# Two rounded halves of an activation as one moving operand of 512 columns: the down and value products of a two-block transformer kernel

## The chip, the cores and the metric

The kernel runs on one core of a Trainium2 chip (trn2), in one launch. The metric is the device time in microseconds of that core. A lower number is better.

## The reference

Two blocks run one after the other on 256 tokens of width 1024, all in float32. The first has two layers of SwiGLU feed-forward, a mixer (a state-space mixer in layer 0, latent attention in layer 1) and a second feed-forward. The second has two layers of a recurrent mixer followed by a sparse feed-forward with 16384 experts. What the change touches are the products that end the four feed-forwards and the two expert layers:

```
def swiglu(h, w_gate, w_up, w_down):
    return (jax.nn.silu(h @ w_gate) * (h @ w_up)) @ w_down
...
        act = jax.nn.gelu(jnp.einsum('td,ted->te', hx, u_sel), approximate=False)
        return jnp.einsum('te,ted->td', gx * act, v_sel)
...
        x = x + FFN_RES_WEIGHT * mod[:, 0, 2][:, None, :] * swiglu(
            h, ffn_w_gate[i, 0], ffn_w_up[i, 0], ffn_w_down[i, 0])
```

`w_down` is 2816 x 1024. The kernel computes the expert layer densely: all 16384 rows of `peer_v` are multiplied, with a routing weight that is zero for most.

## The kernel before

Activations lie transposed: `x` is 8 tiles (d = 0 to 7) of 128 features by 256 tokens. All large weights come as one stream of blocks of 128 x 1024 float32 (512 KB), loaded by SyncE's queue (L480) in a written order into a ring of 4 buffers, or 12 in some stages. To keep float32 accuracy with TensorE's faster fp32r format, every block `W` is split in two: ScalarE rounds it (`split_hi`, L1146, into `weights_hi`, 4 buffers), VectorE computes the rest `W - rounded` in place (`split_lo`, L1641). Activations are split the same way. A product is then three matmuls: rounded x rounded, rounded x rest, rest x rounded.

There are ten stages s = 0 to 9. Each begins with a norm: ScalarE squares the 8 tiles of `x` as they are updated (L1129, waits on `x_upd`), TensorE sums them with a matrix of ones into bank 2 of PSUM (`norm_sum`, L498), ScalarE takes roots, VectorE the reciprocal and the scaled `h`. TensorE meanwhile writes zeros into banks 4 to 7 four times over (`open_acc`, L504, called in `front`), then takes the stage's first blocks.

Stages 0, 2, 3 and 5 are feed-forwards (`ffn`), with 22 pairs of gate and up blocks (`columns_in_parts`, L517, sums in banks 0 and 1 in turn) and then 22 down blocks (`rows_in_parts`, L550). ScalarE takes the silu of a gate sum (L1165), VectorE multiplies it with the up sum (L1674, counts `ffn_a`). For a down block the activation tile is rounded by ScalarE (`gate_hi`, L1159, into `small`) and the rest taken by VectorE (`gate_lo`, L1665, into `work`). VectorE also computes the modulation of later stages here, by products with `mod_weights` blocks (L1569) that POOL's queue loads. How many of these stand between two blocks is set by `products`: 56, 48, 48 and 72 per feed-forward.

Stages 7 and 9 are expert layers (`peer`), with 128 u blocks (L517, banks 0 to 3 in turn; ScalarE's gelu L1482 counts `pe_gelu` and SyncE stores the result to DRAM) and 128 v blocks in a hardware loop of four (`value`, L550). For each v block SyncE reads the activation back (L466), VectorE multiplies it with the routing weights (L2112), ScalarE rounds it (L1476), VectorE takes the rest (L2116). Before the v blocks TensorE writes zeros to banks 4 to 7 once (`open_acc`).

`rows_in_parts` runs over the 8 tiles d and adds three matmuls of 256 columns each to `acc[:, d, :]`, two tiles d per bank, in banks 4 to 7. In the last block of a stage it counts `acc_done` after d = 1, 3, 5. `residual` (L1635) then adds the 8 sums to `x`, times a modulation column, one VectorE instruction per tile, and counts `x_upd` after each. Stages 1, 4, 6 and 8 are the mixers, which the change leaves as they are. In stage 4, POOL's loads of constants and attention weights wait for all `x_upd` of stage 3.

Of the kernel before, what the change touches and what calls it, by code (L numbers as in the profile page):

```python
# [7 lines left out]
F32 = mybir.dt.float32  # L8
F32R = mybir.dt.float32r
# [260 lines left out]
def build(nc, stream, mods, cols_d, consts_d, x_d, pos_d, wuq_d, wukv_d, cond_d, keys_d, pool_d, lora_d, gup_d, vup_d, acts_d, out_d):  # L270
    with ExitStack() as ctx:
# [33 lines left out]

        work, (_, gat_lo) = sb_twice("work", [P, 2048], [([P, 1024], F32), ([P, 4, T], F32R)])

        small, (gat_hi, _) = sb_twice("small", [P, 5, T], [([P, 4, T], F32R), ([P, T], F32)])
        ijg, rs, rv = small[:, 0:3, :], small[:, 3, :], small[:, 4, :]
        PS = ctx.enter_context(nc.psum_tensor("psum", [P, 8, 512], F32))  # L310
        acc = PS[:, 4:8, :].rearrange("p b (s t) -> p (b s) t", s=2)
        sil = work[:, 0:1024].rearrange("p (b t) -> p b t", b=4)
        gat = work[:, 1024:2048].rearrange("p (b t) -> p b t", b=4)
# [175 lines left out]
        def _(pe):  # L489
# [10 lines left out]

            def open_acc():

                for b in range(4):
                    pe.matmul(PS[:, 4 + b, :], zeros[:, :], rep(zeros[:, :], 4), start=True, stop=False, skip_group_check=True)  # L504

# [39 lines left out]

            def rows_in_parts(w, wl, hi, lo, last=False):

                for d in range(DT):
                    for lhs, rhs in ((w, hi), (w, lo), (wl, hi)):
                        mm = pe.matmul(acc[:, d, :], lhs[:, d, :], rhs, start=False, stop=False, skip_group_check=True)  # L550
                    if last and d in (1, 3, 5):
                        mm.then_inc(sem["acc_done"], 1)
                mm.then_inc(sem["block_used"], 1)

            def ffn(s, f):
                base = BASE["ffn", f]
                front(s, ((PS[:, 0, 0:T], True), (PS[:, 0, T:2 * T], False), (PS[:, 1, 0:T], True)))
                for k in range(1, FT):
                    if k >= 2:
                        pe.wait_ge(sem["ffn_a"], FT * f + k - 1)  # L560
                    for half_ in range(1 if k == 1 else 0, 2):
                        w, wl = parts(base + 2 * k + half_)
                        columns_in_parts(PS[:, k % 2, half_ * T:(half_ + 1) * T], w, wl)
                for j in range(FT):
                    w, wl = parts(base + 2 * FT + j)
                    pe.wait_ge(sem["gate_lo"], GATES["ffn", f] + j + 1)
                    rows_in_parts(w, wl, gat_hi[:, j % 2, :], gat_lo[:, j % 4, :], j == FT - 1)

# [467 lines left out]
            def peer(l):  # L1036
# [40 lines left out]
                pe.wait_ge(sem["pe_wev"], T // 4 * (l + 1))  # L1077
                open_acc()

                def value(k, i, last=False):  # L1080
                    w, wl = parts(v0 + k, i)
                    pe.wait_ge(sem["gate_lo"], i * 4 + (GATES["uv", l] + k + 1))
                    rows_in_parts(w, wl, gat_hi[:, k, :], gat_lo[:, k, :], last)

# [455 lines left out]
        def _(dve):  # L1540
# [84 lines left out]
            def residual(s, last):  # L1625

                if s + 1 in FIRST:
                    for p in range(2):
                        split_lo(FIRST[s + 1] + p)
                for d in range(DT):  # L1630
                    if s in BY_ROWS and d < 6:
                        dve.wait_ge(sem["acc_done"], 3 * BY_ROWS.index(s) + d // 2 + 1)
                    else:
                        ready(last(d | 1))
                    dve.scalar_tensor_tensor(x[:, d, :], acc[:, d, :], modc[:, s, 16 + d:17 + d], x[:, d, :], ALU.mult, ALU.add)\  # L1635
                       .then_inc(sem["x_upd"], 1)

# [776 lines left out]
```

## Time and profile before

| | us |
|---|---|
| three timed runs | 3477.92, 3483.32, 3486.91 (median 3483.32) |
| span of the profiled execution, first to last instruction | 3476.7 |
| its own device time | not given apart; the three timed runs lie 1.2 to 10.2 above the span |
| TensorE busy with matmuls, of the span | 3342.0 (96%) |
| TensorE loading weights | 3203.1 (92%) |
| VectorE, ScalarE, POOL busy | 2579.5 (74%), 1608.5 (46%), 198.7 (6%) |
| mean granted TensorE clock | 0.987 of full speed |

How to read it: matmuls are pipelined, so the length that the profile shows for one (about 0.28 us) overlaps the next. What a matmul costs in a stream is the distance from one start to the next. In the chain of work that ended last, a piece "PE psum L550 x504" counts 504 records, matmuls and weight loads as the chain passes through them; its length over its count is the pace of one matmul.

### The profile page before, as it was taken

How to read it: one execution, taken by the hardware profiler on the slowest of the kernel's cores; microseconds unless marked ns; L12 is line 12 of the kernel's file. 1: busy time of each engine (PE TensorE's matmuls, PEld its weight loads, DVE VectorE, ACT ScalarE, POOL GpSimd, SP SyncE). 2: the span in 40 equal slices, each digit the busy share in tenths (PEclk: the TensorE clock that was granted, in tenths of full speed). 3: DMA queues.
4: the chain of work that ended last, by engine and by line, in shares of the span. 5: the costliest groups of instructions: out<-in, count | busy, mean ns of one | idle time of the engine just before them, and what ended most of it. 6: DMA issues, size and time to landing. Idle time of an engine off the chain costs nothing.

```text
span 3476.7 us, 68787 instructions
## 1 busy us (share of the span) xinstructions
PE 3342.0 (96%) x26804; PEld 3203.1 (92%) x26804; DVE 2579.5 (74%) x4576; ACT 1608.5 (46%) x2594; POOL 198.7 (6%) x331
## 2 busy tenths in 40 slices
PE   6999989999999998999999999999899999999998
PEld 5999869999967998889999999998789999999998
DVE  7889667888736896746977867776755977777776
ACT  3456644454445445134444444444414445444444
POOL 1100001101000220200000000000300000000000
PEclk9999999999999999999999999999999999999999
DMA  9964218979613993034664466665215665456665
GB/s 369 359 221 169 74 49 324 336 261 334 249 46 113 385 374 127 31 132 171 228 207 169 166 225 229 230 229 174 75 46 171 230 221 175 169 203 229 232 228 181
DMA packets 246578, 707.46 MB, mean 203 GB/s; under 512 B 27472, under 2 KB 93008, under 8 KB 244928
## 3 DMA queue, kind: packets, MB, share of 16 engines
q1 hardware_dynamic: 212112, 571.64, 47.2%
q0 software_dynamic: 34224, 132.46, 10.2%
q8 instruction: 167, 2.74, 0.3%
q14 instruction: 75, 0.61, 0.1%
HBM read 669.40 MB, written 34.60 MB: 202 GB/s over the span
## 4 chain that ended last, share of the span: by engine, by line
PE 85%; DVE 7%; DMA 4%; ACT 2%; issue 2%; SPq 0%; POOL 0%; DVEq 0%; ACTq 0%; POOLq 0%
PE psum L517 39%; PE psum L550 26%; PE psum L1074 3%; DMA ring<-stream 2%; PE psum L896 2%; PE psum L1009 1%; PE psum L647 1%; DVE ring L1641 1%; PE psum L916 1%; PE psum L498 1%; PE psum L529 1%; DMA arena<-mod_weights 1%; PE psum L530 1%; DVE arena L1569 1%; ACT weights_hi L1146 1%
## 5 line engine op out<-in xcount | busy, mean ns | idle before, releaser
L517 PE MATMUL psum<-hh,weights_hi 128*128 128x256 f32 x4216 | 1212.2, 288 | 19.2 <-ACT arena L1360 8.1
L1146 ACT ACTIVATE weights_hi<-ring 128x1024 fp32r<-128x1024 f32 x711 | 752.0, 1058 | 993.6 <-DMA ring<-stream 928.6
L517 PE MATMUL psum<-h,weights_hi 128*128 128x256 f32 x4216 | 1197.5, 284 | 0.0
L1641 DVE TENSOR_TENSOR ring<-ring,weights_hi 128x1024 fp32r<-128x1024 f32 x711 | 870.1, 1226 | 440.0 <-ACT weights_hi L1146 434.9
L517 PE MATMUL psum<-hh,ring 128*128 128x256 f32 x2976 | 845.5, 284 | 0.0
L517 PEld LDWEIGHTS psum<-hh,weights_hi 128*128 128x128 f32 x4216 | 814.2, 193 | 26.8 <-issue 11.3
L517 PEld LDWEIGHTS psum<-h,weights_hi 128*128 128x128 f32 x4216 | 814.1, 193 | 0.3
L550 PE MATMUL psum<-small,weights_hi 128*128 128x256 f32 x2752 | 774.5, 281 | 4.9 <-DVE work L1665 3.3
L550 PE MATMUL psum<-work,weights_hi 128*128 128x256 f32 x2752 | 772.1, 281 | 0.0
L550 PE MATMUL psum<-small,ring 128*128 128x256 f32 x2304 | 646.1, 280 | 0.0
L517 PEld LDWEIGHTS psum<-hh,ring 128*128 128x128 f32 x2976 | 574.9, 193 | 0.0
L550 PEld LDWEIGHTS psum<-small,weights_hi 128*128 128x128 f32 x2752 | 518.9, 189 | 7.6 <-issue 5.3
L550 PEld LDWEIGHTS psum<-work,weights_hi 128*128 128x128 f32 x2752 | 519.0, 189 | 0.0
L550 PEld LDWEIGHTS psum<-small,ring 128*128 128x128 f32 x2304 | 434.0, 188 | 0.0
L517 PE MATMUL psum<-hh,more_lo 128*128 128x256 f32 x1240 | 351.5, 283 | 0.0
L1641 DVE TENSOR_TENSOR more_lo<-arena,weights_hi 128x1024 fp32r<-128x1024 f32 x214 | 261.1, 1223 | 75.2 <-ACT weights_hi L1146 72.3
L1569 DVE SCALAR_TENSOR_TENSOR arena<-arena 128x1024 f32<-128x1024 f32 x232 | 281.7, 1219 | 11.4 <-DMA arena<-mod_weights 11.1
L1146 ACT ACTIVATE weights_hi<-arena 128x1024 fp32r<-128x1024 f32 x214 | 225.0, 1053 | 114.3 <-PE psum L517 87.0
L517 PEld LDWEIGHTS psum<-hh,more_lo 128*128 128x128 f32 x1240 | 238.7, 193 | 0.0
L2101 DVE TENSOR_SCALAR work<-kept,small 128x128 f32<-128x128 f32 x512 | 142.6, 342 | 83.0 <-PE psum L1074 77.5
L2112 DVE TENSOR_TENSOR work<-work,arena 128x256 f32<-128x256 f32 x256 | 159.1, 623 | 0.0
L2183 POOL DMA_DIRECT2D arena<-mod_weights x208 | 109.8, 528 | 575.8 <-DVE arena L1569 572.3
(410 smaller groups left out, 3897.0 us busy)
## 6 DMA issues: line engine op xcount, KB each, us to landing
ring<-stream SPq DMA_DIRECT2D x735, 512.0 KB, 3.6
arena<-mod_weights POOLq DMA_DIRECT2D x224, 512.0 KB, 6.3
arena<-stream SPq DMA_DIRECT2D x222, 512.0 KB, 5.7
acts<-small SPq DMA_DIRECT2D x256, 128.0 KB, 2.2
work<-acts SPq DMA_DIRECT2D x256, 128.0 KB, 2.2
arena<-cond_rows POOLq DMA_DIRECT2D x3, 1024.0 KB, 7.6
arena<-w_uq POOLq DMA_DIRECT2D x1, 3072.0 KB, 10.3
arena<-constants POOLq DMA_DIRECT2D x2, 1200.0 KB, 5.7
```

What stands on the lines that cost most here:

```text
L498: mm = pe.matmul(PS[:, 2, 0:T], ones, SQ[:, d, :], start=(d == 0), stop=(d == DT - 1))
L517: mm = pe.matmul(out, lhs[:, d, :], rhs[:, d, :], start=(d == 0 and p == 0), stop=(d == DT - 1 and p == 2))
L529: pe.matmul(out, w[:, d, :], h_hi[:, d, :], start=opens and d == 0, stop=False, skip_group_check=True)
L550: mm = pe.matmul(acc[:, d, :], lhs[:, d, :], rhs, start=False, stop=False, skip_group_check=True)
L896: mm = pe.matmul(PS[:, (4 * st + b) % 8, j * P:(j + 1) * P], lhs[:, c, :], rhs[:, c, :], start=True, stop=True)
L1074: mm = pe.matmul(PS[:, 4 + g % 4, j * P:(j + 1) * P], OHI[:, g % 2, j, :], OHJ[:, g % 2, j, :], start=True, stop=True)
L1146: act.activation(whi[:, NTH[n] % WS, :], raw(n), ACT.Copy).then_inc(sem["block_hi"], 1)
L1569: return dve.scalar_tensor_tensor(PRODUCT[:, m % 2, :], block, 1.0, COND[:, 0 if g < 6 else 1, :], ALU.mult, ALU.mult, accum_out=modc[:, g ...
L1641: dve.tensor_tensor(low(n), raw(n), whi[:, NTH[n] % WS, :].bitcast(F32), ALU.subtract)\
L2101: dve.tensor_scalar(OHI[:, g % 2, j, :], iota, ijg[:, 0, t:t + 1], ijg[:, 2, t:t + 1], ALU.is_equal, ALU.mult)
L2112: dve.tensor_tensor(gat[:, k % 4, :], sil[:, k % 4, :], WALL[:, :, i * 4 + k], ALU.mult).then_inc(sem["pe_gated"], 1)
L2183: pool.dma_start(MODRING[slot], mods[i * MOD_RING + (first + slot + MOD_RING)]).then_inc(mod_full[slot], 16)
```

## The change

In the second products (down and v), the rest and the rounded part of an activation lie side by side as one operand `pair` of two tiles of 256 columns. One matmul with the rounded weights multiplies both, into a whole bank of 512: the rest's product in its first half, the rounded part's in its second. A second matmul of 256 columns adds rest-of-weights x rounded activation to the second half. Each tile d has a bank of its own, so the eight sums fill all eight banks, in the order 2, 0, 1, 3, 4, 5, 6, 7. The feed-forward's first down block opens the banks itself (`start`) and first waits for the last `ffn_a`, since banks 0 and 1 held the gate and up sums. The expert layer waits for all `pe_gelu` and then writes zeros to eight banks in place of four. `residual` adds both halves of a bank: for two tiles the first halves, a wait on its own chain, then the second halves. The tiles `work` and `small` become views of one tile `desk`; the data stay in the same places.

```diff
-        work, (_, gat_lo) = sb_twice("work", [P, 2048], [([P, 1024], F32), ([P, 4, T], F32R)])
-
-        small, (gat_hi, _) = sb_twice("small", [P, 5, T], [([P, 4, T], F32R), ([P, T], F32)])
+        desk, (_, gat_parts, _) = sb_twice("desk", [P, 2048 + 5 * T], [([P, 1024], F32), ([P, 8, T], F32R), ([P, T], F32)])
+        work, small = desk[:, 0:2048], desk[:, 2048:2048 + 5 * T].rearrange("p (a t) -> p a t", t=T)
+        gat_lo, gat_hi = gat_parts[:, 0:4, :], gat_parts[:, 4:8, :]
...
+        def acc_parts(d):
+            return PS[:, (2, 0, 1, 3, 4, 5, 6, 7)[d], :]
...
-            def open_acc():
+            def open_acc(first=4):
 
-                for b in range(4):
-                    pe.matmul(PS[:, 4 + b, :], zeros[:, :], rep(zeros[:, :], 4), start=True, stop=False, skip_group_check=True)
+                for b in range(first, 8):
+                    pe.matmul(PS[:, b, :], zeros[:, :], rep(zeros[:, :], 4), start=True, stop=False, skip_group_check=True)
...
-            def rows_in_parts(w, wl, hi, lo, last=False):
+            def rows_in_parts(w, wl, pair, opens=False, last=False):
 
                 for d in range(DT):
-                    for lhs, rhs in ((w, hi), (w, lo), (wl, hi)):
-                        mm = pe.matmul(acc[:, d, :], lhs[:, d, :], rhs, start=False, stop=False, skip_group_check=True)
+                    pe.matmul(acc_parts(d), w[:, d, :], pair, start=opens, stop=False, skip_group_check=True)
+                    mm = pe.matmul(acc_parts(d)[:, T:2 * T], wl[:, d, :], pair[:, 1, :], start=False, stop=False, skip_group_check=True)
...
                     pe.wait_ge(sem["gate_lo"], GATES["ffn", f] + j + 1)
-                    rows_in_parts(w, wl, gat_hi[:, j % 2, :], gat_lo[:, j % 4, :], j == FT - 1)
+                    if j == 0:
+                        pe.wait_ge(sem["ffn_a"], FT * (f + 1))
+                    rows_in_parts(w, wl, gat_parts[:, j % 4:4 + j % 2 + 1:4 + j % 2 - j % 4, :], j == 0, j == FT - 1)
...
                 pe.wait_ge(sem["pe_wev"], T // 4 * (l + 1))
-                open_acc()
+                pe.wait_ge(sem["pe_gelu"], NK * (l + 1))
+                open_acc(0)
...
-                    rows_in_parts(w, wl, gat_hi[:, k, :], gat_lo[:, k, :], last)
+                    rows_in_parts(w, wl, gat_parts[:, k:4 + k + 1:4, :], False, last)
...
-                for d in range(DT):
-                    if s in BY_ROWS and d < 6:
-                        dve.wait_ge(sem["acc_done"], 3 * BY_ROWS.index(s) + d // 2 + 1)
+                def add(d, out):
+                    return dve.scalar_tensor_tensor(x[:, d, :], out, modc[:, s, 16 + d:17 + d], x[:, d, :], ALU.mult, ALU.add)
+
+                for d in range(0, DT, 2):
+                    if s in BY_ROWS:
+                        if d < 6:
+                            dve.wait_ge(sem["acc_done"], 3 * BY_ROWS.index(s) + d // 2 + 1)
+                        else:
+                            ready(last(d | 1))
+                        add(d, acc_parts(d)[:, 0:T])
+                        link(add(d + 1, acc_parts(d + 1)[:, 0:T]))
+                        for k in range(2):
+                            add(d + k, acc_parts(d + k)[:, T:2 * T]).then_inc(sem["x_upd"], 1)
                     else:
                         ready(last(d | 1))
-                    dve.scalar_tensor_tensor(x[:, d, :], acc[:, d, :], modc[:, s, 16 + d:17 + d], x[:, d, :], ALU.mult, ALU.add)\
-                       .then_inc(sem["x_upd"], 1)
+                        for k in range(2):
+                            add(d + k, acc[:, d + k, :]).then_inc(sem["x_upd"], 1)
```

On TensorE, where the first feed-forward's down blocks begin, the order before is this (L517 the last up block, L550 the first down block; `small` holds the rounded activation, `work` its rest, `ring` the rest of the weights):

```order
L517 MATMUL psum<-hh,more_lo 128x256
L550 MATMUL psum<-small,weights_hi 128x256 [waits gate_lo,block_lo]
L550 MATMUL psum<-work,weights_hi 128x256
L550 MATMUL psum<-small,ring 128x256
L550 MATMUL psum<-small,weights_hi 128x256
L550 MATMUL psum<-work,weights_hi 128x256
```

and of the change this:

```order
L521 MATMUL psum<-hh,more_lo 128x256
L553 MATMUL psum<-desk,weights_hi 128x512 [waits ffn_a,gate_lo,block_lo]
L554 MATMUL psum<-desk,ring 128x256
L553 MATMUL psum<-desk,weights_hi 128x512
L554 MATMUL psum<-desk,ring 128x256
```

Two matmuls stand where three stood, and the first waits for `ffn_a` too. On VectorE, the first feed-forward's residual is 8 instructions before:

```order
L1635 SCALAR_TENSOR_TENSOR x<-psum,modc,x 128x256 [waits acc_done] x6
L1635 SCALAR_TENSOR_TENSOR x<-psum,modc,x 128x256 [waits block_used] x2
```

and 16 in the change, of which the first eight (two pairs of tiles) are

```order
L1638 SCALAR_TENSOR_TENSOR x<-psum,modc,x 128x256 [waits acc_done]
L1638 SCALAR_TENSOR_TENSOR x<-psum,modc,x 128x256
L1638 SCALAR_TENSOR_TENSOR x<-psum,modc,x 128x256 [waits dve_chain]
L1638 SCALAR_TENSOR_TENSOR x<-psum,modc,x 128x256
L1638 SCALAR_TENSOR_TENSOR x<-psum,modc,x 128x256 [waits acc_done]
L1638 SCALAR_TENSOR_TENSOR x<-psum,modc,x 128x256
L1638 SCALAR_TENSOR_TENSOR x<-psum,modc,x 128x256 [waits dve_chain]
L1638 SCALAR_TENSOR_TENSOR x<-psum,modc,x 128x256
```

Each pair waits once more, for its own first halves. On TensorE before the v blocks, the four matmuls `L504 MATMUL psum<-zeros 128x512 x4` become eight that wait for `pe_gelu`.

## Rows read from the trace of the kernel before

**Rows 1.** The page: busy time, and the chain that ended last by line

```profile
PE 3342.0 (96%) x26804; PEld 3203.1 (92%) x26804; DVE 2579.5 (74%) x4576; ACT 1608.5 (46%) x2594; POOL 198.7 (6%) x331
...
PE psum L517 39%; PE psum L550 26%; PE psum L1074 3%; DMA ring<-stream 2%; PE psum L896 2%; PE psum L1009 1%; PE psum L647 1%; DVE ring L1641 1%; PE psum L916 1%; PE psum L498 1%; PE psum L529 1%; DMA arena<-mod_weights 1%; PE psum L530 1%; DVE arena L1569 1%; ACT weights_hi L1146 1%
```

**Rows 2.** The chain in order of time: start us, length us, piece

```profile
171.14 59.15 PE psum L550 x504
```

**Rows 3.** Timeline of TensorE, full clock: start us, length, what, count, [idle before <-releaser]

```profile
236.87 3.62 PE L504 MATMUL psum<-zeros 128*128 128x512 bf16 x16
...
1458.94 3.24 PE L904 MATMUL psum<-arena 128*128 128x64 f32 x28
```

**Rows 4.** Timeline of TensorE in stage 5, after an idle stretch, at half clock

```profile
1265.04 0.55 PE L550 MATMUL psum<-small,weights_hi 128*128 128x256 f32 x1 [2.66 <-DVE work L1665]
1265.39 0.41 PE L550 MATMUL psum<-work,weights_hi 128*128 128x256 f32 x1
...
1268.15 0.29 PE L550 MATMUL psum<-small,more_lo 128*128 128x256 f32 x1
```

**Rows 5.** Windows of down and v blocks (stages 0, 5, 7): us, busy by engine

```profile
171.10:230.30 59.20, 59.20 (x507) 59.20 (x506) 50.83 (x77) 28.77 (x42) 6.33 (x12) 1.00 0.69 260
...
1250.00:1324.40 74.40, 70.60 (x579) 69.89 (x577) 67.54 (x107) 34.23 (x51) 11.08 (x21) 0.98 0.76 286
2025.70:2381.90 356.20, 356.20 (x3002) 355.74 (x3003) 262.02 (x376) 171.82 (x251) 0.00 (x0) 1.00 0.69 231
```

**Rows 6.** Timeline, end of stage 0 and start of stage 1

```profile
231.18 3.22 DVE L1635 SCALAR_TENSOR_TENSOR x<-psum,modc,x 128x256 f32<-128x256 f32 x8
...
233.31 3.72 PE L498 MATMUL psum<-arena,kept 128*128 128x256 f32 x16 [0.22 <-ACT arena L1129]
```

**Rows 7.** The same at the ends of stages 7 and 9, and two chained VectorE instructions

```profile
2388.43 3.22 DVE L1635 SCALAR_TENSOR_TENSOR x<-psum,modc,x 128x256 f32<-128x256 f32 x8
...
2389.42 3.72 PE L498 MATMUL psum<-arena,kept 128*128 128x256 f32 x16 [1.81 <-ACT arena L1129]
...
3459.94 3.22 DVE L1635 SCALAR_TENSOR_TENSOR x<-psum,modc,x 128x256 f32<-128x256 f32 x8 [2.99 <-PE psum L550]
...
3461.85 3.61 PE L498 MATMUL psum<-arena,kept 128*128 128x256 f32 x16
...
3467.80 0.42 DVE L1559 SCALAR_TENSOR_TENSOR arena<-small 128x256 f32<-128x256 f32 x1
3468.26 0.43 DVE L1560 TENSOR_TENSOR arena<-arena,small 128x256 f32<-128x256 f32 x1
```

**Rows 8.** The chain in order of time at the end of stage 3

```profile
938.18 3.15 DVE x L1635 x8
...
943.21 15.49 DMA arena<-constants
```

**Rows 9.** Timeline, first down block: last evacuation on VectorE, stages 0 and 5

```profile
170.97 0.28 PE L550 MATMUL psum<-small,weights_hi 128*128 128x256 f32 x1
...
171.95 0.42 DVE L1674 TENSOR_TENSOR arena<-work,psum 128x256 f32<-128x256 f32 x1
...
1256.59 0.28 PE L550 MATMUL psum<-small,weights_hi 128*128 128x256 f32 x1
...
1261.87 0.41 DVE L1674 TENSOR_TENSOR arena<-work,psum 128x256 f32<-128x256 f32 x1
```

**Rows 10.** Timeline, from the u blocks to the v blocks in stage 7

```profile
2020.78 1.04 PE L504 MATMUL psum<-zeros 128*128 128x512 bf16 x4
2022.24 0.39 PE L550 MATMUL psum<-small,weights_hi 128*128 128x256 f32 x1 [0.42 <-DVE work L2116]
...
2022.67 0.38 ACT L1482 ACTIVATE small<-psum 128x256 f32<-128x256 f32 x1 [0.93 <-DMA acts<-small]
```

**Rows 11.** Timeline, one v block in stage 7: its load, and VectorE's last step for it

```profile
2199.90 0.43 SPq L480 DMA_DIRECT2D ring<-stream  x1
...
2206.50 0.42 DVE L2116 TENSOR_TENSOR work<-work,small 128x256 fp32r<-128x256 f32 x1
```

## The prediction

> **What bounds the kernel.** I read the page first [rows 1]: TensorE is busy for 96% of the span, and the chain that ended last runs for 39% through the matmuls of `columns_in_parts` (L517) and for 26% through those of `rows_in_parts` (L550), the ones changed. So time taken from L550 is time taken from the end, wherever TensorE is what the others wait for. Next the windows of those blocks [rows 5]: in stages 0 and 7 TensorE is busy for the whole window, VectorE for 86% and 74% of it. In stage 5 VectorE is busy for 67.5 of 74.4 us and TensorE has gaps: there VectorE sets the pace. Last the pace of one matmul. In down blocks the chain passes 504 in 59.15 us [rows 2], 0.1174 us each; in v blocks 3002 fill 356.2 us [rows 5], 0.1187 each.
>
> **Is that pace columns or something else?** The whole case hangs on this. After 2.66 us without work TensorE ran at half clock (1.2 of 2.4 GHz); there the same matmuls stand 0.212 us apart, 13 steps between 1265.39 and 1268.15 [rows 4]. That is 256 columns at one per cycle with nothing beside. At full clock the columns alone would take 0.107, yet the pace is 0.117 to 0.119. A charge added to each matmul, or a slow column stream, would show at half clock too; it doesn't. What remains is another process beside the columns that takes about 0.117: the weight load that precedes each matmul. A matmul of 64 float32 columns gives the same picture: 28 of them in 3.24 us [rows 3], at most 0.116 each for a quarter of the columns. And a matmul of 512 columns shows the case in which the weight load hides: 16 in 3.62 us, 4 in 1.04 [rows 3, 10], so 12 more in 2.58, 0.215 each (0.226 if the last one's tail is counted in). I take 0.216. It is bf16, not fp32r, but the half-clock row says that fp32r columns too go at one per cycle.
>
> **Term 1, the matmuls.** Per tile d, three of 0.1174 (0.3522) become one of 0.216 and one of 0.1174 (0.3334), since the second still has a weight load as long as itself under it: 0.0188 saved. In v blocks 0.3561 becomes 0.3347: 0.0214. Stages 0, 2 and 3 have 3 x 22 blocks of 8 tiles, 528: 9.9 us. The two expert layers have 2 x 128 x 8 = 2048: 43.8 us. Stage 5 is VectorE's, so I count only its last five blocks, 0.8. Together 54.5 us. Bounds: nothing if 512 columns cost twice the pace of 256; if the second matmul came down to the 0.110 of the 64-column row with its tail of 0.28 taken off, 0.326 per tile and some 76 us. The rows are nearest to the middle value.
>
> By the Trainium skill, TensorE: Matmul & The Clock Gate, section on the back-to-back issue gap, a warm matmul costs N/2.4 + 2.5 ns: three of 256 then cost 327.6 ns, one of 512 and one of 256 325.0. By that rule the change saves 2.6 ns per tile, under 7 us in all, and the sum would come out slower. The rows don't agree with it here: 117.4 ns where it says 109.2.
>
> **Term 2, the residual.** Six stages end by rows. VectorE adds 8 tiles in 3.22 us [rows 6, 7], 0.403 each; the change makes that 16, and 4 waits on its own chain, each 0.46 - 0.40 = 0.06 us by the two chained instructions of [rows 7]. It lasts 6.7 us, 3.5 more. The last tiles count `x_upd` only at the end, and behind each stand a square on ScalarE and a sum on TensorE (about 0.47 each). So the norm's sums end some 7.9 us after the first add. Before, they ended at 237.03 in stage 0, 5.9 after the first add at 231.18 [rows 6]: ScalarE had been late, and part of the delay is hidden by that. Stages 0, 2 and 5 end alike: 2.0 each. Stage 7 had its sums done at 2393.14, 4.7 after 2388.43 [rows 7]: 3.2. Stage 9 is released by TensorE's last block itself, 2.4 by the same count with its sums 5.5 after 3459.94. In stage 3 the chain goes from the last add straight to POOL's 15.49 us load [rows 8]: the full 3.5. Sum 15.1. While it lasts, TensorE has only a sum to do per 0.8 us; the zeros of `front` come after it and nothing else is late.
>
> **Term 3, opening the feed-forward's banks.** The first down block now waits for the last `ffn_a`. In stage 0 it began at 170.97, and that multiplication ran from 171.95 to 172.37 [rows 9]: 1.4 us, and the same in stages 2 and 3, sum 4.2. Nothing hides it, as TensorE is the bound. In stage 5 VectorE has products queued ahead: block 0 began at 1256.59, the multiplication ended at 1262.28 [rows 9]. TensorE then stands for 5.7 us, and by [rows 4] restarts at half clock for 3.1 us. Block 0 ends near 1266.5, and VectorE, which took the rest for block 2 so that TensorE could go on at 1265.04 [rows 4], must wait for that end: about 2.4 us late. The 2.66 us gap shown there is filled in return, so nothing more is lost.
>
> **Term 4, opening the expert layer's banks.** TensorE must wait for the last gelu. In stage 7 that is the instruction from 2022.67 to 2023.05, which waited for a store; the zeros had begun at 2020.78 [rows 10]. TensorE then stands 2.2 us. Near 2.66 us of that the clock fell [rows 4], so I take half clock: eight zeros last some 3.1 us in place of 1.73. The first v block begins at 2026.2 and not 2022.24: 4.0 late. Of this 0.6 is given back, since the second block began only at 2025.70, where the window starts [rows 5], though the first could end at 2025.1. So 3.4 per layer, 6.8 for both (4.0 if the clock holds).
>
> **Sum.** 54.5 saved, 15.1 + 4.2 + 2.4 + 6.8 = 28.5 added: 26.0 less. The span of 3476.7 becomes 3450.7. The median of the runs lies 6.6 above the span; taken from 3483.3 the forecast is 3457. A measurement of this kernel tells 0.3% from no change, 10 us.
>
> The free parts: ScalarE's work is unchanged, SyncE's order too; the views on `desk` cost nothing. Cover that must hold: in v blocks the load issued at 2199.90 ended with VectorE's last step for that block at 2206.92, 7.0 us later [rows 11]. Three blocks pass meanwhile: 8.5 us before, 8.0 after. One microsecond is left.
>
> **Rivals.**
> A, slower. The mechanism: fp32r columns stream no faster than 0.117 per 256 at full clock, so that one of 512 costs 0.235 and the pair what the three did. The place is every L553 matmul. It decides from 0.226 per 512-wide matmul on: there the gain is 28 us and equals the costs. At 0.235 nothing is saved and 28.5 us stay: 3512. For it speaks that no fp32r matmul wider than 256 is in the trace; against it the half-clock pace. The page's gap rule named above also ends on this side, by another way (no weight load to hide), at about 3505, and shares its chance. 15%.
> B, faster still. With two weight loads where there were three, the second matmul falls to 0.110, and the clock holds in the expert layers: 76 saved, 25.7 added, 3433. For it speaks the 64-column row, against it that a load and a matmul of 256 keep running side by side. 10%.
> C, no change. TensorE is faster than its supply: VectorE would be busy for 50.8 of 55.4 us in stage 0, and the v blocks have the microsecond named above, against loads that land unevenly. If stalls take 22 us, half of the v blocks' gain, the time is 3479. Against it speaks that VectorE and ScalarE wait rather than lag in stage 7 [rows 5]. 13%.
> My forecast, 62%.
>
> **Numbers.** The range goes from B's end, 3434, to just past C, 3480; it leaves out A and little more. Faster by over 0.3% (under 3473): the forecast, B and some of C, 0.75. Slower (over 3494): nearly all of A, 0.14. The rest, 0.11.
>
> **What would show it.** L553 matmuls followed by L554 about 0.216 later, and by the next L553 0.117 after that; the v window of 125 blocks down from 356 to some 335 us; the residual x16 at 6.7 us; first sums of the next stage later by 2 to 3.5 us; first down block 1.4 us after the last up block; eight zeros after the last gelu. A step of 0.235 for the wide matmul would make the forecast wrong by its whole gain, and TensorE waits on VectorE or ScalarE inside the v blocks would show C.

## The result, and the profile after

| | before | changed |
|---|---|---|
| median of five timed runs, us | 3481.69 (3477.92 to 3486.91) | 3499.12 (3493.69 to 3503.56) |
| ratio | | 1.0046, 95% interval 1.0035 to 1.0057 |
| profiled execution: span, mean granted clock | 3476.7, 0.987 | 3501.5, 0.984 |

The change costs 17 us where 26 were to be gained. The page of the changed kernel, with its busy line, the chain by line, and the two groups that took the place of L550:

```profile
PE 3342.6 (95%) x24060; PEld 3071.3 (88%) x24060; DVE 2602.0 (74%) x4624; ACT 1610.7 (46%) x2594; POOL 198.7 (6%) x331
...
PE psum L521 36%; PE psum L553 16%; PE psum L554 8%; PE psum L1080 3%; DMA ring<-stream 3%; DMA arena<-mod_weights 2%; PE psum L902 2%; PE psum L1015 1%; PE psum L653 1%; DVE ring L1658 1%; DVE arena L1576 1%; DVE x L1638 1%; PE psum L922 1%; ACT weights_hi L1153 1%; DVE more_lo L1658 1%
...
L553 PE MATMUL psum<-desk,weights_hi 128*128 128x512 f32 x2752 | 965.5, 395 | 10.7 <-DVE arena L1691 8.4
...
L554 PE MATMUL psum<-desk,ring 128*128 128x256 f32 x2304 | 644.0, 280 | 0.0
```

Against [rows 1], TensorE has 2744 matmuls fewer and is busy as long (3342.6 us for 3342.0). The share of the chain in the changed products is 24% for 26%. The matmuls that are left must each take longer, and the timeline of TensorE in stage 0 shows how much longer:

```profile
189.48 0.39 PE L553 MATMUL psum<-desk,weights_hi 128*128 128x512 f32 x1
189.71 0.28 PE L554 MATMUL psum<-desk,more_lo 128*128 128x256 f32 x1
189.83 0.39 PE L553 MATMUL psum<-desk,weights_hi 128*128 128x512 f32 x1
...
190.52 0.39 PE L553 MATMUL psum<-desk,weights_hi 128*128 128x512 f32 x1
```

Three pairs take 190.52 - 189.48 = 1.04 us, 0.347 each (0.3467 over longer stretches). The wide matmul is followed by the narrow one 0.23 later (0.2292 over many), that by the next wide one 0.12 (0.1175) later. The forecast had 0.216 and 0.1174. The windows of the down blocks of stage 0 and of the v blocks of stages 7 and 9 (columns as in [rows 5]):

```profile
172.40:233.40 61.00, 60.98 (x352) 53.68 (x352) 52.04 (x78) 29.85 (x43) 6.33 (x12) 1.00 0.68 249
2047.70:2403.50 355.80, 355.21 (x2028) 309.09 (x2027) 262.18 (x376) 173.04 (x253) 0.00 (x0) 1.00 0.72 232
3122.00:3483.90 361.90, 361.54 (x2049) 312.61 (x2048) 264.22 (x381) 173.47 (x254) 0.00 (x0) 1.00 0.70 226
```

From their first start to their last, all 22 down blocks take 60.97 us, for 61.84 before. All 128 v blocks take 359.6 in stage 7 and 361.9 in stage 9, for 365.1 and 365.2. The 1024 pairs alone would be 1024 x 0.3467 = 355.0. Most of what lies between is in the view of the waits of TensorE's weight loads, for the v blocks of stage 7 and then of stage 9:

```profile
PEld psum L553 <- DVE desk L2133: 5.0, 16, 0.5
...
PEld psum L553 <- DVE desk L2133: 7.0, 26, 0.5
```

The kernel before has 0.4 us of such waits in the v blocks of stage 9 and none in those of stage 7:

```profile
PEld psum L550 <- DVE work L2116: 0.4, 2, 0.3
```

So nearly 12 us of stalls on VectorE's rest of the activation (L2133) are new in the expert layers of this execution, which was the slowest of the five. The size is not steady. The kernel below that leaves out the first halves has the same v blocks, and in its whole run it waits less:

```profile
PEld psum L553 <- DVE desk L2131: 5.4, 17, 0.5
```

Its v blocks took 359.2 and 356.3 us. Next the places where banks are opened, in the timeline of TensorE (stages 0, 5, 7 and 9):

```profile
172.42 0.47 PE L553 MATMUL psum<-desk,weights_hi 128*128 128x512 f32 x1 [1.39 <-DVE arena L1691]
...
1277.40 0.77 PE L553 MATMUL psum<-desk,weights_hi 128*128 128x512 f32 x1 [4.19 <-DVE arena L1691]
...
1278.18 0.63 PE L553 MATMUL psum<-desk,weights_hi 128*128 128x512 f32 x1
...
1278.82 0.63 PE L553 MATMUL psum<-desk,weights_hi 128*128 128x512 f32 x1
...
2042.41 1.89 PE L508 MATMUL psum<-zeros 128*128 128x512 bf16 x8 [1.52 <-ACT desk L1489]
2043.94 0.59 PE L553 MATMUL psum<-desk,weights_hi 128*128 128x512 f32 x1
...
3119.06 3.50 PE L508 MATMUL psum<-zeros 128*128 128x512 bf16 x8 [2.27 <-ACT desk L1489]
3122.00 0.87 PE L553 MATMUL psum<-desk,weights_hi 128*128 128x512 f32 x1
```

Each wait stands where the forecast put it: on the last multiplication (L1691, L1674 before) and on the last gelu (L1489). In stage 7 the zeros kept full clock after 1.52 us of idleness; in stage 9, after 2.27, they ran at half clock and cost 3.50 us. Stage 5 restarts at half clock too: a pair every 0.64 us, which is 768 columns at 1.2 GHz and nothing on top. The end of stage 0, on VectorE and TensorE:

```profile
231.85 6.87 DVE L1638 SCALAR_TENSOR_TENSOR x<-psum,modc,x 128x256 f32<-128x256 f32 x16
...
233.93 1.13 PE L502 MATMUL psum<-arena,kept 128*128 128x256 f32 x4 [0.26 <-ACT arena L1136]
...
238.82 1.13 PE L502 MATMUL psum<-arena,kept 128*128 128x256 f32 x4 [0.56 <-ACT arena L1136]
```

The residual takes 6.87 us for 3.22 [rows 6], and the norm's last sum ends at 239.95 for 237.03. In stage 3 the late residual moves POOL's load, in the chain:

```profile
955.35 15.40 DMA arena<-constants
```

It began at 943.21 [rows 8]: 12.1 us later. Put together by stage, all in us, against the same points of the kernel before:

| stage | late at its start | opening adds | blocks save | after them added |
|---|---|---|---|---|
| 0 | 0 | 1.4 | 0.9 | 2.3 |
| 2 | 4.4 | 1.4 | 0.9 | 2.5 |
| 3 | 7.5 | 1.4 | 0.9 | 4.1 |
| 5 | 13.4 | 4.2, and 3.1 in the gate and up blocks ahead | 2.1 | 2.4 |
| 7 | 20.8 | 0.9 | 5.5 | 3.1 |
| 9 | 21.5 | 4.0 | 3.3 | 2.6 |

By this table 13.6 us are saved; openings add 13.3, residuals 17.0. Together they make 16.7. The two profiled spans differ by 24.8. Of the rest, 3.1 are stage 5's gate and up blocks and 4.7 the mixer stages, which the change doesn't touch. Executions scatter by as much (the profiled one was 4.4 above its median), and the experiments, which go by medians, don't need it.

### The profile page after: what moved, and what is told of

It reads as the page before. It is cut to its first block, busy times and chain, and to the rows that moved or that the text cites. A ratio compares the mean times of both kernels' runs of the same rounds, so it can differ in the third digit from the quotient of the medians.

```text
span 3501.5 us, 63349 instructions
## 1 busy us (share of the span) xinstructions
PE 3342.6 (95%) x24060; PEld 3071.3 (88%) x24060; DVE 2602.0 (74%) x4624; ACT 1610.7 (46%) x2594; POOL 198.7 (6%) x331
## 4 chain that ended last, share of the span: by engine, by line
PE 79%; DVE 9%; DMA 7%; ACT 3%; issue 3%; SPq 0%; DVEq 0%; POOL 0%; POOLq 0%; ACTq 0%
PE psum L521 36%; PE psum L553 16%; PE psum L554 8%; PE psum L1080 3%; DMA ring<-stream 3%; DMA arena<-mod_weights 2%; PE psum L902 2%; PE psum L1015 1%; PE psum L653 1%; DVE ring L1658 1%; DVE arena L1576 1%; DVE x L1638 1%; PE psum L922 1%; ACT weights_hi L1153 1%; DVE more_lo L1658 1%
## 5 line engine op out<-in xcount | busy, mean ns | idle before, releaser
L553 PE MATMUL psum<-desk,weights_hi 128*128 128x512 f32 x2752 | 965.5, 395 | 10.7 <-DVE arena L1691 8.4
L554 PE MATMUL psum<-desk,ring 128*128 128x256 f32 x2304 | 644.0, 280 | 0.0
L553 PEld LDWEIGHTS psum<-desk,weights_hi 128*128 128x128 f32 x2752 | 517.9, 188 | 137.5 <-DVE desk L2133 11.9
L554 PEld LDWEIGHTS psum<-desk,ring 128*128 128x128 f32 x2304 | 432.8, 188 | 0.1
L1576 DVE SCALAR_TENSOR_TENSOR arena<-arena 128x1024 f32<-128x1024 f32 x232 | 282.0, 1220 | 13.3 <-DMA arena<-mod_weights 12.9
L2118 DVE TENSOR_SCALAR desk<-kept,desk 128x128 f32<-128x128 f32 x512 | 142.8, 344 | 82.8 <-PE psum L1080 76.9
L2129 DVE TENSOR_TENSOR desk<-desk,arena 128x256 f32<-128x256 f32 x256 | 158.5, 621 | 1.8 <-PE psum L554 1.8
L1080 PE MATMUL psum<-desk 128*128 128x128 f32 x1024 | 131.3, 274 | 0.4 <-DVE desk L2119 0.3
L554 PE MATMUL psum<-desk,more_lo 128*128 128x256 f32 x448 | 126.3, 282 | 0.0
```

The lines of the kernel that those rows point to most:

```text
L553: pe.matmul(acc_parts(d), w[:, d, :], pair, start=opens, stop=False, skip_group_check=True)
L554: mm = pe.matmul(acc_parts(d)[:, T:2 * T], wl[:, d, :], pair[:, 1, :], start=False, stop=False, skip_group_check=True)
L1080: mm = pe.matmul(PS[:, 4 + g % 4, j * P:(j + 1) * P], OHI[:, g % 2, j, :], OHJ[:, g % 2, j, :], start=True, stop=True)
L1576: return dve.scalar_tensor_tensor(PRODUCT[:, m % 2, :], block, 1.0, COND[:, 0 if g < 6 else 1, :], ALU.mult, ALU.mult, accum_out=modc[:, g ...
L2118: dve.tensor_scalar(OHI[:, g % 2, j, :], iota, ijg[:, 0, t:t + 1], ijg[:, 2, t:t + 1], ALU.is_equal, ALU.mult)
L2129: dve.tensor_tensor(gat[:, k % 4, :], sil[:, k % 4, :], WALL[:, :, i * 4 + k], ALU.mult).then_inc(sem["pe_gated"], 1)
```

## The experiments

Each ratio is against runs of the kernel before in the same set; it is taken over the runs and can differ from the quotient of the two medians, by up to 1.6 us. Its interval is 3 to 5 us to each side. The changed kernel was timed in a set of its own, so differences to it are between medians of two sets; the kernel before moved by 0.9 us between that set and the first five experiments' (3481.69, 3480.82), and by 2.0 to that of the last set (3479.66).

**What sets the pace of a matmul?** A kernel that computes nothing of the reference sends streams of 48 or more equal matmuls with nothing beside, then the same beside VectorE's work and beside loads.

```
for k in range(48):   # widths 256, 320, 384, 512; 128 or 64 weight columns; fp32r and bf16
    pe.matmul(PS[:, k % 4, 0:512], wk(k), xc[:, 0:512], ...)
```

> Computes nothing of the reference; it runs only streams of 48 matmuls of one form each on a core where nothing else runs, and then two more streams of 512 fp32r columns, during which VectorE subtracts 128x1024 tiles (first) and eight blocks of 512 KB are loaded (second). In the changed kernel a 512-wide fp32r matmul took 0.229 us and a 256-wide one 0.117. Theory S (the fp32r columns themselves stream at some 0.44 ns each at full clock): 512 columns take 0.226 to 0.230 in the quiet core too, 384 about 0.173, 320 about 0.145, 256 about 0.117, and a weight load of 64 columns in place of 128 changes nothing. Theory L (each load of fp32r weights takes some 13 ns of the array that nothing hides): 512 take 0.229 and 256 take 0.120 with 128 weight columns, but about 7 ns less with 64. Theory C (other engines and loads take SBUF reads away): 512 take 0.216 in the quiet core and 0.229 only beside VectorE or the loads. bf16 takes 0.216 and 0.109 in all of them.

The timeline of TensorE in that kernel (L78 to L90 the widths, L84 the operand in two pieces, L93 and L96 with 64 weight columns, L101 in bf16, L104 with the same weights each time, L107 beside VectorE; L110, beside the loads, is as long as L107):

```profile
19.60 6.10 PE L78 MATMUL psum<-xr,wr 128*128 128x256 f32 x48
...
30.55 11.26 PE L81 MATMUL psum<-xr,wr 128*128 128x512 f32 x48
...
46.66 11.26 PE L84 MATMUL psum<-xr,wr 128*128 128x512 f32 x48
...
62.76 8.68 PE L87 MATMUL psum<-xr,wr 128*128 128x384 f32 x48
...
88.52 11.41 PE L93 MATMUL psum<-xr,wr 128*64 128x512 f32 x48
...
104.77 5.81 PE L96 MATMUL psum<-xr,wr 128*64 128x256 f32 x48
...
125.97 5.40 PE L101 MATMUL psum<-xb,wb 128*128 128x256 bf16 x48
...
136.20 11.28 PE L104 MATMUL psum<-xr,wr 128*128 128x512 f32 x48
147.32 21.92 PE L107 MATMUL psum<-xr,wr 128*128 128x512 f32 x96
```

From 256 to 384 to 512 columns a stream grows by 2.58 us twice, 0.42 ns per column: one column per cycle at 2.4 GHz. So the columns aren't slow. The long stream gives the pace itself: (21.92 - 0.39) / 95 = 0.2266 for 512, of which the columns are 0.2133. That leaves 0.0133 per matmul, and the same on top of 256 columns: their records in the trace stand 0.120 apart. The charge is there in the wide matmul as in the narrow one: nothing hides it. It is the same with the operand in two pieces, the same weights each time, VectorE busy beside, or loads running. Slow columns and contention fall; a charge per matmul stands. The 64-column case was predicted to lose half of the charge; at 256 it does (0.1133), at 512 it doesn't (11.41 us is more than 11.26).

**Is the charge set by the weight load?** A second kernel of the same kind varies the weight columns, and runs the kernel's own sequences of three and of two matmuls.

> Computes nothing of the reference: streams of 48 matmuls of one form each. The first such run gave, in a quiet core at full clock, 120.0 ns for 256 fp32r columns, 173.3 for 384 and 226.7 for 512: one column per cycle and 13.3 ns more per matmul; with weights of 64 columns 256 took 113.3, 6.7 more than its columns. Theory L (a charge per matmul that goes with the columns of its weights, 0.104 ns each, and is not hidden under a longer matmul): 96 weight columns give 116.7, 32 give 110.0, 64 with 384 columns about 166.7 and 32 with 512 about 216.7; the kernel's order of three narrow matmuls gives 360 per tile and the changed pair 346.7. Rival (a charge of 13.3 for every fp32r matmul, and the 113.3 an accident of that form): 120 for 96 and 32 weight columns. The changed kernel's saving per tile would be 13.3 by both, more than the 5 ns seen in the kernel, so what the pair and the triple take here also says whether the kernel's own 351 is a special case of the order (weights twice the same, rest and rounded part in turn).

Its timeline: two starts of the sequence of three, two of the sequence of two (and a narrow matmul, L84, of it), then streams of 48 (L87 all into one bank, L90 with 96, L93 and L96 with 32, L99 with 64 weight columns):

```profile
20.80 0.28 PE L78 MATMUL psum<-xr,wr 128*128 128x256 f32 x1
...
21.88 0.28 PE L78 MATMUL psum<-xr,wr 128*128 128x256 f32 x1
...
31.75 0.39 PE L83 MATMUL psum<-xr,wr 128*128 128x512 f32 x1
...
33.16 0.40 PE L83 MATMUL psum<-xr,wr 128*128 128x512 f32 x1
33.40 0.28 PE L84 MATMUL psum<-xr,wr 128*128 128x256 f32 x1
...
42.05 6.10 PE L87 MATMUL psum<-xr,wr 128*128 128x256 f32 x48
...
52.99 5.93 PE L90 MATMUL psum<-xr,wr 128*96 128x256 f32 x48
...
63.77 6.01 PE L93 MATMUL psum<-xr,wr 128*32 128x256 f32 x48
...
74.62 11.47 PE L96 MATMUL psum<-xr,wr 128*32 128x512 f32 x48
...
90.94 8.66 PE L99 MATMUL psum<-xr,wr 128*64 128x384 f32 x48
```

Three matmuls take (21.88 - 20.80) / 3 = 0.360, the pair (33.16 - 31.75) / 4 = 0.353. With nothing beside, the change saves some 7 ns per tile, half of the 13.3 that one charge less would give: here the narrow matmul starts 0.24 after the wide one, and not 0.2266, so part of the charge comes back where the two alternate.

In the large kernel the saving is as small, 0.3520 in down blocks against 0.3467 or 5.3 ns, but it is made up otherwise. There the pair has its two charges and no more (0.3200 of columns and 0.0267), and it is the three narrow matmuls that take less than 0.360. Why they do, no run shows.

The rows on the weight columns were missed. 96 columns fit; 32 columns don't: 6.01 us where 0.110 a matmul, some 5.6 us, was expected, and at 512 the stream of 32 columns is slower than that of 128, 11.47 for 11.26. A charge in proportion to the weight load is refuted too. What it is stays open. Its size in such streams, and that a wide matmul doesn't hide it, are measured.

**What do the fewer matmuls bring by themselves?** The changed kernel, with the wide matmul cut in two of 256 into the same bank. All openings and residuals stay.

```diff
-                    pe.matmul(acc_parts(d), w[:, d, :], pair, start=opens, ...)
+                    pe.matmul(acc_parts(d)[:, 0:T], w[:, d, :], pair[:, 0, :], start=opens, ...)
+                    pe.matmul(acc_parts(d)[:, T:2 * T], w[:, d, :], pair[:, 1, :], start=False, ...)
```

> The change with its wide matmul cut into two of 256 columns, into the same halves of the same banks; waits, banks and residual stay. If the wide matmul is a gain, only smaller than forecast (0.346 per pair against 0.352 to 0.356), the down blocks of a feed-forward go back to 61.8 us and the v blocks to 365 us, and the time is about 12 us above the change's 3499: 3511. If the wide matmul itself is what makes the change slower (by stalls that it brings), the time is the change's or less.

Measured: 3513.35 (3508.62 to 3515.86), 1.0097 of the kernel before (1.0084 to 1.0111), whose median was 3480.82. That is 14.2 us above the changed kernel by the medians (17.8 by the two ratios): the whole worth of term 1, pace and stalls together. The windows of its down blocks of stages 0 and 2 and of its v blocks of stages 7 and 9 (columns as in [rows 5]):

```profile
172.10:234.80 62.70, 62.62 (x527) 62.65 (x528) 52.19 (x79) 29.95 (x44) 6.34 (x12) 1.00 0.67 243
683.50:745.50 62.00, 61.92 (x527) 61.95 (x528) 49.84 (x73) 29.82 (x44) 5.28 (x10) 1.00 0.69 236
2047.40:2412.60 365.20, 365.20 (x3073) 364.83 (x3072) 267.08 (x380) 174.94 (x254) 0.00 (x0) 1.00 0.71 229
3128.50:3489.30 360.80, 360.78 (x3073) 360.55 (x3072) 264.92 (x381) 173.50 (x254) 0.00 (x0) 1.00 0.70 226
```

The expectation had 61.8 us for the down blocks and 365 for the v blocks. Stages 2 and 7 fit; stages 0 and 3 took 62.6 and stage 9 took 360.8, less than with the wide matmul in the profiled execution above. So three narrow matmuls have two paces, 0.3520 and 0.3560 us per tile, at full clock, and can hold either through a whole stage. The pair has one, 0.3467. The kernel before ran its first three feed-forwards at the lower and its v blocks at a mixture. Which pace a stage gets, no run settles. Against the one the pair saves 5.3 ns per tile, against the other 9.3. The column of savings in the table above, from one execution of each kernel, could therefore come out otherwise by 0.7 us in a feed-forward and 4 in an expert layer.

**What do the first halves cost?** The first eight additions of each residual are left out, so the product of the weights' rounded part with the activation's rest is computed but is missing from the result.

```diff
-                        add(d, acc_parts(d)[:, 0:T])
-                        link(add(d + 1, acc_parts(d + 1)[:, 0:T]))
```

> The change with a residual that adds only the second halves of the banks: the product of the rounded weights with the rest of the activations is computed and left out of the result. Theory (the doubled residual lies on the path): 3.5 us less at the end of stage 3 and 2 to 3 at five others, 14 to 17 in all, so 3482 to 3485. Rival (ScalarE's squares and table load cover most of it): 8 or less, 3491 or more.

Measured: 3481.84 (12 runs, 3472.85 to 3487.67), 1.0001 (0.9991 to 1.0012). That is 17.3 us less than the changed kernel (15.7 by the ratios), and the residual is back at its old length, in VectorE's timeline:

```profile
231.64 3.22 DVE L1638 SCALAR_TENSOR_TENSOR x<-psum,modc,x 128x256 f32<-128x256 f32 x8
```

**What do the openings cost?** The kernel before, with the two waits and the eight zeros and nothing else of the change.

```diff
+                    if j == 0:
+                        pe.wait_ge(sem["ffn_a"], FT * (f + 1))
...
+                pe.wait_ge(sem["pe_gelu"], NK * (l + 1))
-                open_acc()
+                open_acc(0)
```

> The kernel before with only the waits of the change: the first down block waits for the last ffn_a, and in the expert layers all gelus are awaited before zeros go to eight banks. Theory: 1.4 us in stages 0, 2 and 3 each, 2 to 4 in stage 5, 2 to 3.4 per expert layer, 10 to 15 in all over the kernel before. Rival: later waits absorb most of it, 5 or less.

Measured: 3495.91 (3492.76 to 3500.83), 1.0048 (1.0034 to 1.0062), 15.1 us more (16.7 by the ratio). Its timeline has idle times in the same places as the changed kernel's (5.67 us in stage 5), and the same two kinds of zeros:

```profile
172.18 0.36 PE L550 MATMUL psum<-small,weights_hi 128*128 128x256 f32 x1 [1.38 <-DVE arena L1677]
...
2036.12 1.89 PE L504 MATMUL psum<-zeros 128*128 128x512 bf16 x8 [1.82 <-ACT small L1485]
...
3111.63 3.47 PE L504 MATMUL psum<-zeros 128*128 128x512 bf16 x8 [2.10 <-ACT small L1485]
```

Not all of it is idle time: its down blocks of stages 0, 2 and 3 ran at the higher of the two paces, 62.62 us each for 61.84, which is 2.3 us, and its v blocks took 1.4 us less than before.

The three runs close the account: 17.3 + 15.1 - 14.2 = 18.2 us, where 3499.12 - 3480.82 is 18.3, and 17.4 by the changed kernel's own set. That the medians agree so well is partly luck, as each difference is uncertain by 4 us and more. By the ratios it is 15.7 + 16.7 - 17.8 = 14.6 for 16.0.

**Can the openings be had for nothing?** The changed kernel with another order of banks: those that the gate and up sums (or the last u block) held come last, and TensorE waits only when it gets to them. The first v block opens its banks itself, so the zeros go.

```diff
-            return PS[:, (2, 0, 1, 3, 4, 5, 6, 7)[d], :]
+            return PS[:, ((2, 4, 5, 6, 7, 0, 1, 3) if s in (7, 9) else (2, 3, 4, 5, 6, 7, 0, 1))[d], :]
...
+                    if opens and d == opens[0]:
+                        pe.wait_ge(sem[opens[1]], opens[2])
```

> The change with its banks taken in another order: in the feed-forwards banks 2 to 7 first and 0, 1 last, with the wait for the last ffn_a in the middle of the first down block (before its seventh tile); in the expert layers bank 2 first and 3 last, no matmuls of zeros, the first v block opens the banks itself, and the last gelu is awaited before its last tile. If the opening waits cost 15 us and nothing else takes their place: 1.4 less in stages 0, 2 and 3, 2 in stage 5, 2 to 3.5 per expert layer, 11 in all, 3488. Rival (the wait only moves, since the work behind it is late anyway): 3495 or more.

Measured: 3485.92 (12 runs, 3478.21 to 3492.17), 1.0018 (1.0007 to 1.0029) of a median before of 3479.66. That is 6.3 us above the kernel before, where the changed one was 17.4: the openings gave back 11 to 13 of the 15.1 us, by the one or the other way of taking the difference. What stays is mainly stage 5, where VectorE multiplies the last sum only after its queued products; TensorE does six tiles, then stands for 3.50 us in place of 4.19:

```profile
1268.71 0.50 PE L555 MATMUL psum<-desk,weights_hi 128*128 128x512 f32 x1 [3.50 <-DVE arena L1693]
...
1270.45 0.63 PE L555 MATMUL psum<-desk,weights_hi 128*128 128x512 f32 x1
...
1271.09 0.63 PE L555 MATMUL psum<-desk,weights_hi 128*128 128x512 f32 x1
```

It goes on at full clock, and 1.2 us later the granted clock falls to half: from there a pair takes 0.64 us.

**And the first halves?** On top of that, the last block of a stage is done in narrow matmuls that all go to the second halves. So the first halves are complete one block earlier, and VectorE adds them while TensorE does the last block. The splits of the next stage's first two blocks come after the residual. One of POOL's loads also counts another semaphore; the load itself is the same.

```diff
+                    if last:
+                        pe.wait_ge(sem["lo_add"], 8 * BY_ROWS.index(s) + d + 1)
+                        for k in range(2):
+                            pe.matmul(acc_parts(d, s)[:, T:2 * T], w[:, d, :], pair[:, k, :], start=False, ...)
...
+                    for d in range(DT):
+                        if d < 6:
+                            dve.wait_ge(sem["acc_done"], 6 * b + d // 2 + 1)
+                        ...
+                        add(d, acc_parts(d, s)[:, 0:T]).then_inc(sem["lo_add"], 1)
```

> As v1_banks_late, and the last block of each stage adds its rest product to the second half by narrow matmuls, so that the first halves are complete a block earlier and VectorE adds them during the last block (TensorE waits, tile by tile, for that read); the next stage's two splits of weights follow the residual. Theory (of the doubled residual's 17 us nearly all can be hidden): 14 to 16 less than v1, so about 3472, below the kernel before (3481) by what the wide matmuls give less small change. Rival (VectorE has no room in the last two blocks, or the splits come late): within 5 us of v1, 3483 to 3488.

Measured: 3467.29 (12 runs, 3463.95 to 3476.88), 0.9964 (0.9954 to 0.9974). This beats both kernels: 12.4 us below the kernel before, 18.6 below the kernel with the late banks in the same set, where 14 to 16 were forecast, and some 30 below the changed one. The timeline of VectorE and TensorE at the end of stage 0:

```profile
227.45 6.48 DVE L1647 SCALAR_TENSOR_TENSOR x<-psum,modc,x 128x256 f32<-128x256 f32 x16
...
232.42 3.72 PE L502 MATMUL psum<-arena,kept 128*128 128x256 f32 x16 [0.22 <-ACT arena L1143]
```

The sixteen additions are all there, but begin 4.4 us earlier, and the sums run in one piece as in [rows 6]. What is left, 12.4 us, is near the 14.2 of term 1. By their noise the two could differ by several us, so that nothing finer can be read from them; stage 5's wait of 3.50 us, for one, is still there.

## Why the prediction was wrong

**The step that failed** is in term 1, after the sentence on the half-clock row: "What remains is another process beside the columns that takes about 0.117: the weight load", and from it that a matmul of 512 columns is "the case in which the weight load hides". The half-clock row was read rightly (no charge at 1.2 GHz) and concluded from wrongly. The sentence "A charge added to each matmul, or a slow column stream, would show at half clock too" is false for the charge: the pair in stage 5 of the changed kernel has none at half clock (0.64 us for 768 columns) and 0.0267 at full clock. The row excludes slow columns, but doesn't say that the charge lies beside the columns and so can be covered by more of them. At full clock the charge comes on top at every width: 0.2266 for 512 columns, of which 0.2133 are columns. The row taken for the size, 0.215, was of bf16 zeros; the text noted the other format and set it aside by the half-clock row. In bf16 the charge is small indeed: in streams at 256 columns a matmul took 0.109 us for fp32r's 0.120. The 64-column row pointed to the load, but the two small kernels show that the charge doesn't follow the load.

**Term 1 in numbers.** Forecast 54.5 us, measured 14.2 by the kernel cut in two (17.8 by the ratios, 13.6 by the stages' lengths). The down blocks of stages 0, 2 and 3 were to save 9.9 and saved 2.6. The v blocks were to save 43.8 and saved 8.8: they were forecast at 342.7 us a layer and took 359.6 and 361.9. Of the 36 us between, 2 x (355.0 - 342.7) = 24.6 are the pace of the pair, 0.3467 for 0.3347. Nearly all of the rest are the stalls of TensorE's weight loads on VectorE (5.0 and 7.0 in the waits of this execution), for which the term had nothing. The 0.3561 that it took as the price of three was a mean over two paces and some waits. Stage 5 stands under term 3.

**Term 2, the residual**: right. Forecast 6.7 us a piece and 15.1 in all; measured 6.87, and 17.3 in all (15.7 by the ratios). By stage: 2.3, 2.5 and 2.4 for 2.0 each, 4.1 for 3.5 (stage 3, by the late load), 3.1 for 3.2, and 2.6 for 2.4.

**Term 3, opening the feed-forward's banks**: right in stages 0, 2 and 3, at 1.39 to 1.44 for 1.4. In stage 5 TensorE stood 4.19 us for 5.7 (5.67 in the kernel with the openings alone) and restarted at half clock, as described. The forecast charged 2.4, since a later gap would be filled in return, and gave 0.8 of term 1 back: 1.6 net. Measured are 4.2 added and 2.1 saved: 2.1 net.

**Term 4, opening the expert layer's banks**: 3.4 per layer forecast. Stage 9 added 4.0 with zeros at half clock, stage 7 0.9 with the clock held. The forecast had named both cases (6.8, or 4.0 if the clock holds); one layer fell on each side. Terms 3 and 4 together were 13.4, measured 15.1, of which about one is not openings but the change of pace.

**The sum.** The costs were forecast at 28.5 and measured at 32.4, close enough for the sign. The sign hung on the gain alone, as the prediction said of a wide matmul at 0.235.

**The rivals.** A came true in its direction and its place, every L553 matmul, though not in its mechanism: the columns are fast, a charge isn't covered. The wide matmul stands at 0.229 and not 0.235 (by its own prices 0.235 would still have left 4.9 us in the v blocks, where the text says nothing). Its turning point of 0.226 was too generous: at 0.226 the text gave 28 us of gain, because it took the v blocks' 0.1187 per matmul as the price of a matmul, with nothing set aside for the supply. The rule of the Trainium skill, TensorE: Matmul & The Clock Gate, section on the back-to-back issue gap, gave about 3505 and came nearest to the measured 3499. Its form is what the runs show, columns plus a constant per matmul. For bf16 its figures agree ((5.40 - 0.28) / 47 = 0.109 in the stream of 256). For fp32r the constant is 13.3 ns and not 2.5, so that the rule, too, had the three matmuls of a tile at 327.6 ns where the trace has 352. The prediction set it aside because one of its figures didn't fit, and lost with it the form that did. B didn't happen: the second matmul stayed at 0.117. C's mechanism is there in small: the supply of the v blocks, said to have one microsecond left, gave up about 12 us in two layers of the profiled execution, and less in others, with the pair still far from the 0.3347 that C had assumed. (Its 55.4 us for the down window of stage 0 should have been 56.0 by term 1's prices, which changes nothing.)

## What to carry to other kernels

Before a forecast rests on the pace of an instruction that the trace doesn't have, in its format and its width, measure it in a small kernel: the two sequences side by side would have shown here that three matmuls made two save 7 ns and not 20. What is missing at half clock can still be there at full clock: the row doesn't say what is added there, nor what would be hidden. Where a change pays a little on every block and costs something at each seam, look for the seams first: with the banks taken in the order in which they come free, and the first halves added under the last block, some 30 us of seams went and the small gain was left.

## What the runs showed of the hardware beyond what was expected

- A fp32r matmul with 128 weight columns costs 0.417 ns per moving column and 13.3 ns on top at 2.4 GHz in a stream of its own kind (0.120 for 256, 0.2266 for 512), with the same weights or others, and whether VectorE works beside it or loads run. At 1.2 GHz nothing is on top [rows 4].
- In the large kernel three narrow matmuls of a down or v tile take 0.3520 or 0.3560 us and not 0.360, and keep one of the two for whole stages; the wide and narrow pair takes 0.3467 in every stage of the kernels that have it, wherever nothing holds it up. Not settled.
- With fewer weight columns that doesn't shrink steadily: streams of 48 at 256 columns took 6.10, 5.93, 5.81 and 6.01 us for 128, 96, 64 and 32 weight columns, and at 512 those of 64 and 32 columns (11.41, 11.47) were slower than that of 128 (11.26). Not settled.
- Before the v blocks, the clock was at half after 2.10, 2.27 and 2.59 us without work (eight zeros in 3.47, 3.50 and 3.32 us) and stayed full after 1.52, 1.76, 1.82 and 1.88 (1.89 us each time). In stage 5 of the kernel with the late banks TensorE stood for 3.50 us and restarted at full clock, and the clock fell 1.2 us after the restart. So the fall can come behind the idle stretch. Where it meets the eight zeros, they cost 1.4 to 1.6 us more.
